# A first block reordered: memory keys and values first, queries and keys with tokens on the partitions, heads gated chunk by chunk

## The reference, cut to what matters

```python
h = rms_norm(x, g_mix)
q, k, v, z, xbc, dt = split(h @ w_in)             # 1024 | 1024 | 1024 | 1024 | 2048 | 16
q, k = partial_rope(rms_norm(q, g_q)), partial_rope(rms_norm(k, g_k))   # 16 heads of 64; 16 columns turned
attn = rms_norm(masked softmax attention(q, k, v), g_attn_out)
xbc = silu(causal_conv4(xbc)); dt = softplus(dt + dt_bias)
y = chunked_scan(x, dt, a, B, C) + d_skip * x     # 16 heads of 64, 4 groups, chunks of 128 tokens
ssm = rms_norm_by_group(y * silu(z), g_ssm_out)   # 4 groups of 256
x = x + concat(attn, ssm) @ w_out
q = rms_norm(rms_norm(x, g_cross) @ w_cq, g_cq)   # 4 heads of 128
k, v = split(rms_norm(mem, g_mem) @ w_ckv); k = rms_norm(k, g_ck)       # mem: 256 x 2048
x = x + (softmax(q k^T / sqrt(128)) v) @ w_co
x = x + relu(rms_norm(x, g_mlp) @ w_up)^2 @ w_down
```

## Time and profile before

| | before |
|---|---|
| median of 3 runs | 3931.32 us (3930.61 to 3931.39) |
| profiled execution | 3935.18 us |
| its span, first to last instruction | 3933.4 us |
| mean granted clock of TensorE | 0.926 |
| TensorE matmuls, VectorE, ScalarE, GpSimd busy | 85%, 63%, 35%, 21% of the span |
| read from HBM | 947.58 MB, mean 241 GB/s |

### The profile page before, as it was taken

One profiled execution on the slowest core, in us unless ns is written; L12 is line 12 of the kernel. 1 busy time (PEld: TensorE's weight loads), 2 busy tenths in 40 slices (PEclk: granted clock), 3 DMA queues, 4 the chain that ended last, 5 costly groups with the idle time before them and its releaser, 6 DMA issues.

```text
span 3933.4 us, 53304 instructions
## 1 busy us (share of the span) xinstructions
PE 3335.8 (85%) x21118; PEld 2754.5 (70%) x21118; DVE 2494.0 (63%) x3320; ACT 1386.3 (35%) x1971; POOL 838.4 (21%) x612
## 2 busy tenths in 40 slices
PE   7999789899999999999999997766667667666688
PEld 7888778799999999999998896732222223222248
DVE  5567765655455555875555666977777776555556
ACT  4346444554345443564445543221100001100124
POOL 1000001100000010000000011246565555555521
PEclk9999889999999999999999998888887888888899
DMA  6443235355555556556553465889999999999964
GB/s 208 129 129 108 92 93 160 114 183 188 181 182 183 188 178 198 158 175 187 166 175 121 134 185 192 314 334 422 421 422 421 422 421 420 422 421 422 422 258 144
DMA packets 187594, 953.17 MB, mean 242 GB/s; under 512 B 20817, under 2 KB 21073, under 8 KB 121425
## 3 DMA queue, kind: packets, MB, share of 16 engines
q0 software_dynamic: 73728, 536.90, 33.1%
q1 hardware_dynamic: 112464, 407.68, 33.0%
q10 hardware_dynamic: 1152, 5.17, 0.3%
HBM read 947.58 MB, written 2.10 MB: 241 GB/s over the span
## 4 chain that ended last, share of the span: by engine, by line
PE 61%; DMA 18%; DVE 11%; POOL 4%; ACT 3%; issue 2%; DVEq 0%; ACTq 0%; POOLq 0%; SPq 0%
PE ps L478 61%; DMA BIG<-in_peer_v,CS 6%; DMA HLF<-in_peer_v,CS 6%; DMA HF<-in_peer_v,CS 2%; DVE HL L1526 2%; DMA HLF<-in_peer_u,CS 2%; POOL HLF L465 2%; POOL BIG L465 2%; DMA BIG<-in_peer_u,CS 2%; DVE BIG L1530 1%; DVE BIG L2092 1%; ACT HL L997 1%; ACT BIG L991 1%; DVE BIG L1526 1%; DVE TMP L1530 0%
## 5 line engine op out<-in xcount | busy, mean ns | idle before, releaser
L478 PE MATMUL ps<-HS,HL 128*128 128x256 f32 x11088 | 1460.0, 288 | 41.0 <-DVE HL L1526 29.4
L478 PEld LDWEIGHTS ps<-HS,HL 128*128 128x128 f32 x11088 | 1407.5, 196 | 53.7 <-DVE HL L1526 32.0
L1526 DVE TENSOR_TENSOR HL<-RAW,HL 128x1024 fp32r<-128x1024 f32 (+1 forms) x772 | 949.2, 1230 | 208.4 <-ACT HL L997 144.0
L997 ACT CAST HL<-RAW 128x1024 fp32r<-128x1024 f32 (+1 forms) x772 | 805.4, 1043 | 611.8 <-PE ps L478 565.8
L478 PE MATMUL ps<-BIGR,HL 128*128 128x256 f32 x6528 | 865.8, 284 | 9.1 <-DVE X L1526 4.5
L478 PEld LDWEIGHTS ps<-BIGR,HL 128*128 128x128 f32 x6528 | 824.2, 192 | 15.8 <-issue 6.3
L478 PE MATMUL ps<-BIG,HF 128*128 128x512 f32 (+1 forms) x760 | 396.4, 671 | 188.1 <-DMA BIG<-in_peer_v,CS 165.7
L478 PE MATMUL ps<-HLF,HF 128*128 128x512 f32 x656 | 346.4, 681 | 155.3 <-DMA HLF<-in_peer_v,CS 143.7
L478 PEld LDWEIGHTS ps<-BIG,HF 128*128 128x128 f32 (+1 forms) x760 | 160.5, 221 | 418.0 <-issue 391.1
L448 POOL COPY NSUM<-TMP 128x256 f32<-128x256 f32 x6 | 4.0, 671 | 2035.6 <-ACT TMP L993 2035.6
L2092 DVE CUSTOM_DVE_ANT_0 BIG<-BIG 128x2048 f32<-128x2048 f32 x133 | 304.9, 2293 | 166.6 <-DMA BIG<-in_peer_u,CS 157.8
(11 more groups left out here) (176 smaller groups left out, 2225.4 us busy)
## 6 DMA issues: line engine op xcount, KB each, us to landing
RAW<-in_w_up SPq DMA_DIRECT2D x128, 512.0 KB, 3.8
RAW<-in_w_down SPq DMA_DIRECT2D x128, 512.0 KB, 4.4
RAW<-in_w_out SPq DMA_DIRECT2D x64, 512.0 KB, 3.6
RAW<-in_w_qk SPq DMA_DIRECT2D x32, 512.0 KB, 4.4
RAW<-in_w_xbc SPq DMA_DIRECT2D x32, 512.0 KB, 3.6
RAW<-in_w_xr SPq DMA_DIRECT2D x32, 512.0 KB, 3.7
RAW<-in_w_yr SPq DMA_DIRECT2D x32, 512.0 KB, 3.7
RAW<-in_w_gr SPq DMA_DIRECT2D x32, 512.0 KB, 4.0
```

Of the source, the lines that this page charges most:

```text
L478: return e.matmul(o, l, r, start=start, stop=stop, skip_group_check=True)
L997: s.done(e.copy(o, i), sig)
L1526: v.done(e.tensor_tensor(o, a, b, op), sig)
```

## The change

1. **Order.** w_ck and w_cv come first, then w_v, w_qk, w_dt, w_xbc, w_z, w_out. mem is loaded in four parts between the first units by SP's queue and cut as it lands; x follows, then the positions. GpSimd forms squares of mem's first four chunks and adds four more.
2. **q and k in tokens form.** w_qk is read as 8 blocks, four groups of four heads with a q and a k block each. ScalarE evacuates with the token's factor, `prepared(G)` squares, sums, roots, scales and turns 16 narrow columns with free-dimension broadcasts, and TensorE transposes the result into chunks. The rotation and selection matrices are gone, and so are `norm_rope` and `mem_sums`.
3. **Gating.** Heads and their inputs are two generators beside each other. An attention head starts when its group is ready, a scan head when its two chunks of x are turned. The product with z moves from each head to each chunk in the group norm. Turns of the inputs use bank 3 in place of the shared bank 6, and ScalarE in place of VectorE copies them out.
4. **Ending.** The last group norm and the head norm of w_ck's keys run in w_out; w_out joins LATE, and so does w_ck.
5. **Cross heads** run as the background of w_cq, each after its chunk. The query norm is taken into the exponential's scale: squares, two small sums per head, a root and a reciprocal; the key gain takes both gains. Outputs are cut from the bank directly.

```diff
-LATE = ("w2_ao",)
+LATE = ("w_ck", "w_out", "w2_ao")
...
+LAYERS = [("w_ck", 4, 8, 128, 2, False), ("w_cv", 4, 4, 256, 4, True), ("w_v", 8, 4, 256, 4, True),
+          ("w_qk", 16, 4, 256, 4, True), ("w_dt", 1, 8, 128, 2, False), ("w_xbc", 16, 8, 128, 2, False),
+          ("w_z", 8, 8, 128, 2, False), ("w_out", 16, 8, 128, 2, False), ("w_cq", 4, 8, 128, 2, False),
```

SP's queue:

```diff
+            e.dma_start(VEC[:, :], A["vecs"]).then_inc(s_vec, 16)
+            for i in range(4):
+                e.dma_start(MEM[:, 4 * i:4 * i + 4, :], A["memT"][:, 4 * i:4 * i + 4, :]).then_inc(s_mem[i], 16)
+                e.dma_start(RAW[:, i, :], STREAM[i]).then_inc(s_w[i], 16)
+            e.dma_start(CON[:, :], A["consts"]).then_inc(s_con, 16)
+            for u in range(4, NUNITS):
...
+                if u in (4, 5):
+                    for i in (2 * u - 8, 2 * u - 7):
+                        e.dma_start(X[:, 4 * i:4 * i + 4, :], A["xT"][:, 4 * i:4 * i + 4, :]).then_inc(s_x[i], 16)
```

TensorE (`mem_sum` is called after w_ck's first output):

```diff
+            def mem_sum():
+                pe.wait_ge(s_con, 16)
+                pe.wait_ge(s_padd, PSQ["mem"] + 1)
+                mm(norm_bank[:, 0:T], con("ones"), NSUM[:, :], True, False)
+                for j in range(2):
+                    pe.wait_ge(s_square, SQ["mem"] + j + 1)
+                    for k in range(4):
+                        p = mm(norm_bank[:, 0:T], con("ones"), tmp(j)[:, k, :], False, j == 1 and k == 3)
...
+            def prepared(G):
+                for _ in range(4):
+                    yield
+                for a in range(2):
+                    pe.wait_ge(s_qkr, G + 1)
...
+                    for c in range(2):
+                        for i in range(2):
+                            o = 512 * i + 256 * a + 128 * c
+                            p = tr(PS[3][:, 256 * c + 128 * i:256 * c + 128 * i + 128], TG[G % 2][:, o:o + 128])
+                    p.then_inc(s_turn3, 1)
+                    yield
```

VectorE:

```diff
+            def prepared(G):
+                x = TG[G % 2]
+                h = x.rearrange("p (i a d) -> p i a d", i=2, a=8)
+                v.wait_ge(s_gsq, G + 1)
+                total(SS, TMP[:, 0, :].rearrange("p (a d) -> p a d", d=64), ALU.add, False, (s_gsum, G + 1))
+                yield
+                v.wait_ge(s_grt, G + 1)
+                recip(SS, SS)
+                xa = x.rearrange("p (a d) -> p a d", d=64)
+                tt(xa, xa, SS.unsqueeze(2).to_broadcast([128, 16, 64]), ALU.mult)
+                for i in range(2):
+                    xi = x[:, 512 * i:512 * i + 512].rearrange("p (q h d) -> p q h d", q=2, h=4)
+                    tt(xi, xi, vec("g_qk", 0, 128).rearrange("p (q d) -> p q d", q=2).unsqueeze(2).to_broadcast([128, 2, 4, 64]),
+                       ALU.mult)
+                yield
+                tt(RP[0], h[:, :, :, 0:16], CS4[:, 0, :, :].unsqueeze(2).to_broadcast([128, 2, 8, 16]), ALU.mult)
+                for d in (0, 8):
+                    tt(RP[1][:, :, :, d:d + 8], h[:, :, :, 8 - d:16 - d],
+                       CS4[:, 1, :, d:d + 8].unsqueeze(2).to_broadcast([128, 2, 8, 8]), ALU.mult)
+                tt(h[:, :, :, 0:16], RP[0], RP[1], ALU.add, (s_qkr, G + 1))
```

The generators, the same on TensorE, ScalarE and VectorE, and TensorE's list of layers:

```diff
+            def scan_heads():
+                live, h = [], 0
+                while h < 16 or live:
+                    if h < 16 and ready[0] > 4 + h // 4:
+                        live.append(ssd_head(h))
+                        h += 1
+                    for g in list(live):
+                        if next(g, g) is g:
+                            live.remove(g)
+                    yield
+                    have["ssd"] = h - len(live)
...
+            def inputs():
+                for G in range(4):
+                    yield from until("w_qk", 4 * G + 4)
+                    yield from prepared(G)
+                    ready[0] = G + 1
+                yield from until("w_dt", 1)
+                yield from ssd_pre()
+                yield from ssd_b()
+                yield from attn_norm()
+                for n in range(4):
+                    yield from ssd_x(n)
+                    ready[0] = 5 + n
+                for g in range(4):
+                    yield from until("ssd", 4 * g + 4)
+                    yield from until("w_z", 2 * g + 2)
+                    late[0] = g == 3
+                    yield from ssm_norm(g)
...
+            def mixers():
+                yield from first()
+                begun[0] = True
+                yield from together(heads(), inputs())
...
+            dense(L["w_ck"], mem, lambda c: mem_sum() if c == 0 else None, g_bg)
+            dense(L["w_cv"], mem, None, g_bg)
+            while not begun[0]:
+                next(g_bg)
+            for name in ("w_v", "w_qk", "w_dt", "w_xbc", "w_z"):
+                dense(L[name], normed("g_mix"), None, g_bg)
+            while not attended[1]:
+                next(g_bg)
+            def ending():
+                while not late[0]:
+                    next(g_bg)
+                yield
+                step(g_bg)
+                yield
+                drain(g_bg)
+                yield
+                yield from head_norm("ck")
+            g_end = ending()
+            dense(L["w_out"], mixed, None, g_end)
```

ScalarE, a cross head, and TensorE's call:

```diff
+                while cq[0] <= h:
+                    yield
+                bank_done(L["w_cq"], h)
+                act(tmp(0)[:, h, :], CQ[:, h, :], ACT.Square, (s_cqsq, h + 1))
+                s.wait_ge(s_cqsum, h + 1)
+                act(d[:, 6:8], norm_bank[:, 2 * h:2 * h + 2], ACT.Sqrt, (s_crt, h + 1), bias=con("eps128"))
+                yield
+                s.wait_ge(s_max, n + 1)
...
+                for i in range(2):
+                    act(P[:, i * T:i * T + T], score_bank(k)[:, i * T:i * T + T], ACT.Exp, sig_score(k) if i else None,
+                        bias=d[:, i:i + 1], scale=d[:, 6 + i:7 + i], acc=d[:, 2 + i:3 + i])
...
+            dense(L["w_cq"], normed("g_cross"), evac_cq, g_cr)
+            drain(g_cr)
```

More of the change, by code:

```diff
@@ new lines, in scalar, with ending @@
+            dense(L["w_v"], evac_v, g_bg)
+            dense(L["w_qk"], evac_qk, g_bg)
+            dense(L["w_dt"], None, g_bg)
+            dense(L["w_xbc"], evac_xbc, g_bg)
+            dense(L["w_z"], evac_z, g_bg)
+            while not attended[1]:
+                next(g_bg)
+            def ending():
+                while not late[0]:
+                    next(g_bg)
+                yield
+                step(g_bg)
+                yield
+                drain(g_bg)
+                yield
+                s.wait_ge(s_mxs, 8)
+                bank_done(L["w_ck"], 3)
+                yield from head_norm("ck", CK)
@@ L1819, in vector @@
-            v.wait_ge(s_con, 16)
-            v.wait_ge(s_vec, 16)
-            low(0)
-            low(1)
-            for c in range(4):
-                v.wait_ge(s_x[c], 16)
-            for c in range(15):
-                normed_low("g_mix", c)
-            norm_end("g_mix")
-            g_an = angles()
-            next(g_an)
-            qk, dt = L["w_qk"], L["w_dt"]
-            dense(qk, lambda c: scaled(QK[:, c, :], qk, c), g_an)
-            drain(g_an)
-            g_nr = before()
@@ L1841, in vector @@
+            low(4)
+            low(5)
+            for c in range(8):
+                normed_low("g_mix", c)
+            v.wait_ge(s_nfree, NORM["mem"] + 1)
+            recip(KEEP[:, 0, :], KEEP[:, 0, :], (s_rx, RXN["mem"]))
             g_bg = mixers()
-            dense(L["w_z"], lambda c: scaled(Z[:, c, :], L["w_z"], c), g_bg)
+            dt = L["w_dt"]
             def conv(L, n, o, w, b, sig):
@@ new lines, in vector, with ending @@
+            while not begun[0]:
+                next(g_bg)
+            dense(L["w_v"], None, g_bg)
+            dense(L["w_qk"], None, g_bg)
+            dense(dt, evac_dt, g_bg)
+            dense(L["w_xbc"], evac_xbc, g_bg)
+            dense(L["w_z"], lambda c: scaled(Z[:, c, :], L["w_z"], c), g_bg)
+            while not attended[1]:
+                next(g_bg)
+            def ending():
+                while not late[0]:
+                    next(g_bg)
+                yield
+                step(g_bg)
+                yield
+                drain(g_bg)
+                yield
+                yield from head_norm("ck", CK, 1)
@@ L1886, in vector @@
+                yield
+                v.wait_ge(s_cxhi, h + 1)
+                tt(cx[1][:, h, :], out_bank[:, 0:T], cx[0][:, h, :].bitcast(F32), ALU.subtract,
+                   (s_ofree, OUTS["cross"] + h + 1))
+                yield
+            g_cr = pipeline(cross(h) for h in range(4))
+            dense(L["w_cq"], evac_cq, g_cr)
+            drain(g_cr)
             dense(L["w_co"], residual("g_mlp", L["w_co"]))
@@ L2134, in experts @@
                     if q in gate_at:
[L2135 removed]
+                        while not routed[0]:
                             yield
```

863 lines of the change are left out of this document (489 added, 374 removed).

## The result

The changed kernel takes 3885.4 us (median of four runs, 3882.0 to 3888.1) where the kernel before takes 3931.3 beside it: ratio 0.988, 95% interval 0.987 to 0.990. It is 46 us faster; 80 were forecast. All of it comes from the part ahead of w_up0, whose first unit starts at 696.3 instead of 742.9. From there to the end the two profiles take 3188.3 and 3190.5 us.

What follows compares the result with a forecast made beforehand. TensorE's dense units were taken as the floor up to w_co; excess over them was to fall from 276.3 to 196.3 us, a gain of 80 from 3931.32: 3851.3 us. Own range 3836 to 3868, wide range 3820 to 3890.

Steps and rivals of the forecast that it cites:

- two rivals whose mechanisms did not come: Whole kernel: VectorE sets the pace more than counted, 3881 us, chance 0.18; waits are covered, 3826 us, chance 0.14.
- Start and w_v: Start with w_ck and w_cv: excess 20 us, w_v starting near 66; w_v: excess falls from 31.0 to 0.
- w_qk, w_dt and w_xbc to unit 12: Attention heads and group preparation beside these units: excess 56 us (49 if log1p is covered, 75 if half each chain shows).
- covered with nothing to spare: Group preparation: VectorE's chain of about 11 us set against four units, 11.5 us, so it was taken as hidden.
- The term for log(1 + x): Step sizes' log1p chain at step 37: holds VectorE as before, two units and two score products ahead; 9 us kept.
- the alarm: In w_qk: the forecast is wrong if TensorE waits for VectorE by more than 15 us.
- idle time under 5 us: In w_qk: a sign that the forecast holds, TensorE idle for less than 5 us.
- The rival in which preparation shows: Groups' preparation not hidden: four chains of 11 us stop TensorE, 44 and slow units 10, gain 26, 3905 us; chance 0.05.
- VectorE paces more than I count: Scan units cost 7.46 us in w_xbc (45 for 27.7), w_z goes to 44; gain 50, 3881 us; chance 0.18.
- w_xbc 13 to 21, w_out: Attention norm in w_xbc: excess 13 us (8 to 13); last group norm and w_ck's head norm in w_out: 11 (7 to 15.7).
- Cross heads: Heads 0, 1 and head 2's scores beside w_cq: excess 1.9 + 10 us; head 3 left before w_co: 12.5 (9 to 20).
- Slower than before: TensorE falls to its lower clock between small products and stays; 4026 us if all 68 units are affected; chance 0.03.

Runs made afterwards that it cites:

- the one with the steps set apart: Changed kernel with ScalarE taking an attention head's exponential one step after VectorE's maximum, and VectorE scaling probabilities one step after that: 3870.4 us, ratio 0.985 to the kernel before.

## Why the prediction was right and wrong

**Direction and bound.** Right: faster, inside the range, by the mechanism named, and nothing behind w_up0's first unit moved. But the forecast's own range, 3836 to 3868, was missed by 17 us, and the wide one was met with 5 to spare: it was drawn to take in two rivals whose mechanisms did not come.

**Start and w_v.** Right within 2 us: w_v starts at 67.8 (66 predicted), its 16 units take 46.2 with nothing beside them. The 31.0 us of rope work leave this stage as said.

**w_qk, w_dt and w_xbc to unit 12.** The step that failed. The term was 56 and measured 78.0. Its parts were right apart: a covered preparation costs 1.1 to 1.5 us of transposes in eight units, a head 2.51. Wrong was "beside a unit's low part (1.23) and a head's steps (about 2.4) it stays under 5.39" together with "covered with nothing to spare". It added busy times and checked the preparation's chain against four units, each alone. But both chains go from VectorE to ScalarE and back inside the same step, in engines that work strictly in order, so their lengths add: the unit at 172.7 takes 8.1 us though no engine has 8 us of work in it. Cutting the heads' part of it took 13.2 of the 22 us out of this window; holding the heads back in addition took out 10 more, part of it only moved behind this window.

"Covered with nothing to spare" was right for group 0, but it left nothing for the other three. The term for log(1 + x), 9, was too high: the two units that it held up took 11.2 us, and 8.2 without it, so 3. What the sum had at nothing is unit 9 of w_xbc, 10.8 us where a unit with a head takes 5.4: there the convolution's activation, its two table loads and the heads' exponentials follow each other. That 3 and 5.4 make 8.4, near the 9, is luck.

Of the forecast's two signs for w_qk, the alarm (15 us of waits for VectorE) did not ring, since TensorE waited there only 2.4 us for VectorE and 5.9 for ScalarE; the other, idle time under 5 us, did fail: it was 8.3. In the whole window it waited 9.9 for each, and the rest was the lower clock. The rival in which preparation shows had this mechanism, given 0.05; of its 54 us at most the 22 came.

**The rival with the right number.** "VectorE paces more than I count" gives 3881, 4 us from the result, by a mechanism that did not happen: its loss was to stand in scan units (7.46 a unit in w_xbc, 44 in w_z). They took 5.14 a unit, under the forecast's 5.65, and 30.5. That its number lies nearest is luck. (The forecast's parts of a unit, 3.0 and 1.23 and 1.23 and 0.15, make 5.61 and not 5.65; in ten units that is 0.4 us.)

**w_xbc 13 to 21, w_out.** 4.2 and 5.2 us short. In w_out, the terms that the forecast names, 1.5, 5 and 2.7, make 9.2 and not its 11, so 7.0 are missing by them. Unit 3 lasts 11.8 us (508.1 to 519.9): in it stand w_ck's head norm, with TensorE waiting 3.5 for ScalarE's squares and then busy for 3.6 with the sums, and 1.6 of wait for the last cut. Neither stage was taken apart further.

**Cross heads.** The gap came out at 13.1 (12.5 predicted), w_cq's excess at 14.6 (11.9). The forecast had w_cq and the gap 7.5 us shorter together than before; they are 4.2 shorter, and standing side by side is not shown to bring more than 0.5 of it. w_co, taken as today (36.2), took 38.7; in the other profiles with the same code it takes 36.2 to 38.2, so no cause in the change is shown for it.

**Slower than before.** The lower clock did not stay. It did cost: 0.95 and 0.90 are its share in the term that failed.

## What to carry to other kernels

When background work of several engines shares a step, count for each step the longest path from engine to engine through everything that stands in it, not each engine's busy time and not each chain alone. Where an engine waits inside a step for another engine's answer, put question and answer into different steps if the consumer's step allows it: here that cost no work and no length and gave 15 us in the median, 13.2 in its own window. Then ask whether two such chains must run side by side at all; starting the heads only when they could run without a pause gave another 3.5 in the profile and 5.6 in the medians. And when work is moved to another engine, look at the busy time of the engine that gave it away: here 8.7 us were moved and 2.0 were gone.

Find the unit that is long in the timeline before cutting it: the split of log(1 + x) was aimed at a unit that did not hold it.

## What the runs showed that was not expected

The clock fell or held in the same instructions. In w_cq the instructions of the changed kernel and of the one with the steps set apart are the same, and six units start at the same distances from the first, within 0.1 us (0, 3.0, 8.0, 10.9, 16.5, 20.2 us). The seventh starts at 29.2 in one and at 27.9 in the other, and the mean granted clock up to it is 0.95 and 1.00:

```profile
606.90:636.00 29.10, 25.15 (x182) 23.63 (x181) 15.01 (x24) 17.84 (x27) 0.00 (x0) 0.95 0.32 109
```

```profile
592.90:620.90 28.00, 24.05 (x183) 22.77 (x181) 14.77 (x24) 17.52 (x27) 0.00 (x0) 1.00 0.33 105
```

To w_co it is 50.7 us in one and 47.9 in the other. Ten of the profiles with this form of the stage have one of these two values within 0.1 us, two have 49.2 and 49.3. The scan stretch of w_xbc takes 51.0 to 51.4 or 49.5 to 49.9 in the same way; where it takes the lower value w_z takes 77.9 or 78.0 instead of 76.6, so little of that is left at w_z's end. What decides was not tried; no instruction of the stage differs. An edit is therefore judged in its own stage, and 3 us elsewhere are no evidence for it.
